# Identity products in the opening of a two-block transformer kernel, a first weight part made by GpSimd, and weight parts moved at two hand-overs

## The chip, the cores and the metric

One NeuronCore of a Trainium2 chip runs the whole program. Its engines are TensorE (PE, matmul), VectorE (DVE), ScalarE (ACT), GpSimd (POOL) and SyncE (SP, which here only issues DMAs). The metric is the device time of one execution in microseconds. The kernel before takes 1233.42 us, the median of three runs (1233.16, 1233.42 and 1234.23).

## The reference

Two transformer blocks in float32 over 256 tokens of 1024 features, cut here to what sets the order of the work. The first block has two layers, the second has one.

```python
def first_block(...):
    for i in range(2):
        h = rms_norm(x, g[0])
        m = neighborhood_attention(h, ...) if i == 0 else diff_attention(h, ...)
        x = x + rms_norm(m, g[1])
        f = conv_glu_ffn(rms_norm(x, g[2]), ...)       # D_FF = 2816
        x = x + rms_norm(f, g[3])
        gate = sigmoid(rms_norm(x, g[4]) @ ple_w_gate[i])
        x = x + gate * (p[i] @ ple_w_proj[i])

def second_block(...):                                  # one layer
    h = h + 0.5 * swiglu(rms_norm(h), w1_gate, w1_up, w1_down)
    u = rms_norm(h) @ w_in                              # HGRN2 mixer and latent attention
    h = h + concat([o_hg, o_mla]) @ w_out
    h = h + 0.5 * swiglu(rms_norm(h), w2_gate, w2_up, w2_down)
    h = h + sigmoid(rms_norm(h) @ w_ple_gate) * (p @ w_ple_proj)
    return rms_norm(h, ln_final)
```

## The kernel before

The 256 tokens are two tiles of 128 (t = 0 and 1), and the 1024 features are 8 blocks of 128. The layers run as ten phases, numbered 0 to 9: `na, ffn, ple, da, ffn, ple, glu, mix, glu, ple`. Phase 0 is the neighborhood attention, phase 2 the gate of layer 0, phase 3 the differential attention, phase 4 the FFN after it. The order of every engine's work is written out by hand; counting semaphores tie the engines together.

**Weights.** They are cut into slabs of 1 MB (128 partitions by 2048 elements), numbered through the program. A slab passes four steps. SP issues its DMA into one of 3 `raw` buffers (L524); a buffer is free once the low part of the slab three before it is made (`lo_done`). ACT rounds it to fp32r, the high part `w_hi` (`feed`, L691). DVE subtracts that from the raw values, the low part `w_lo` (`feed`, L1249, or in two halves, `feed_half`, L1257). PE multiplies: each product of float32 accuracy is three fp32r products, high by high, high by low and low by high (L1939 to L1941). `w_hi` and `w_lo` are rings of 5 slabs. An engine's `feed(n)` makes every slab below number n that it has not made yet. `hi_done` counts high parts, `lo_done` low parts.

**Activations.** A tile is normalized in this way: ACT squares and sums it (`pre` before a stage, `post` after one, L695), GpSimd turns the sums into 1/rms (`powers`, L562 to L571), DVE multiplies by it (`normed`, L1288, two instructions of 512 columns), PE transposes the 8 blocks against the identity (`turn_x`, L1996), and then ACT and DVE make the high and the low part of each block (`tile_parts`, L698 and L1271). In `tile_parts` ACT's step i waits for DVE's step i - 2, and step i of DVE waits for that of ACT, so the two alternate. In phases whose rms factor is applied later (4 among them) `turn_x` transposes x itself.

**The opening.** PE runs 16 identity products into a bank that nobody reads (L2601), turns the first gain row (L1961, copied out by DVE at L1860), then both tiles (`turn_x(0, 0)` and `(0, 1)`), and enters `first_columns` (L2108: high part of slab 0 by both parts of the tokens, 2 columns groups of 16 matmuls; L2113: its low part, 16 matmuls), then `half_columns(0, 2)`, `(0, 3)`, scores, taps and `value_rows`. DVE runs: gain copy, `normed(0, 0)`, steps 0 to 3 of tile 0, `normed(0, 1)`, steps 4 to 7, tile 1, `feed(2)` (slabs 0 and 1), `lambdas` and `rotary` (some 4.4 us of small instructions), slab 2, then in `attention0` `expand(0)` (waits for the DMA of the relative-position table), `scores(0, 0)`, `expand(1)`, `taps_out` and slab 3. ACT runs the four squares, steps 0 to 3 of tile 0, slab 0, steps 4 to 7, tile 1, slabs 1 and 2. GpSimd issues late gain rows, makes both 1/rms, sets 32 columns of `invf` (L588, which `rotary` waits for) and, once `hi_done` is 2, issues the DMAs of the table (L579).

**Hand-over from phase 2 to phase 3.** PE makes the last gate quarter in two pieces with `turn_x(3, 0)` between them, and then runs `value_rows(3, 0, 0, 0)` and `(3, 0, 1, 0)` (12 products each on tile 0, four blocks each, waiting for each block's low part), `turn_x(3, 1)` and `value_rows` on tile 1. With b the first gate slab, slabs b+4 and b+5 are those of these value rows, and slab b+6 that of the first columns. `add_gated(2, n)` (DVE, L1324 and L1325) adds gate piece n to x; `gates(2, n)` (ACT, L742) makes its sigmoid. Pieces 2 to 4 belong to tile 1 and end in `pre(3, 1)`.

**End of phase 3.** With b the first slab of phase 3, b+12 to b+15 are those of the output projection, b+16 to b+18 the first three of the FFN. After the last two units of attention (6 and 7) DVE scales the outputs (`scaled_outputs(3, 1)`, L1489 and L1493, which waits for GpSimd's 1/rms of these units, L570 and L571), PE turns them (`output_turn(3, 1)`, L1961), ACT and DVE split them (`output_parts(3, 1)`), and PE runs the second half of the projection, `output_piece(3, 1, t, half)`. ACT's `post(3, 0)` follows its slabs up to b+18; then come the rms factor, `post_added` (DVE, L1314) and `turn_x(4, 0)`, which PE runs before the last 6 products of the projection.

## Time and profile before

| | |
|---|---|
| median of three runs | 1233.42 us (1233.16 to 1234.23) |
| the profiled execution | 1234.14 us, of which the span in the trace is 1232.4 us |
| PE busy | 1210.2 us, 98% of the span |
| DVE busy | 943.8 us, 77% |
| ACT busy | 674.5 us, 55% |
| POOL busy | 135.1 us, 11% |
| DMA | 214.52 MB, mean 174 GB/s |
| chain that ended last | PE 91%, DVE 4%, ACT 3%, DMA 1% |

Times inside the trace are microseconds from the start of the span. A group's idle time before it is named with what ended it. PEclk is the granted TensorE clock: 1.00 is 2.4 GHz, 0.50 is 1.2 GHz. A matmul's record is longer than its distance to the next, since matmuls are pipelined.

### The profile page before, as it was taken

Reading aid. Unit: us, or ns where it says so; the run is one execution under the profiler, and the core shown is the slowest. Engines: PE = TensorE matmul, PEld = TensorE weight load, DVE = VectorE, ACT = ScalarE, POOL = GpSimd, SP = SyncE. Lnnn points to the kernel's source line nnn. Section 1 sums busy time; section 2 is a strip of 40 time slices with the busy share of each in tenths; the row PEclk is TensorE's granted clock in tenths of the full one; section 3 lists DMA queues with packets and bytes.
Section 4 is the critical chain, followed back from the end, with each engine's and each line's share of the span. In section 5 each row is a group of like instructions: output and inputs, shape, how many; then the busy total and the mean of one; then the engine's idle time right before and its main releaser. Section 6 shows DMA issues by size and latency. Waiting matters only on the chain.

```text
span 1232.4 us, 17869 instructions
## 1 busy us (share of the span) xinstructions
PE 1210.2 (98%) x6977; PEld 1054.8 (86%) x6977; DVE 943.8 (77%) x1272; ACT 674.5 (55%) x1064; POOL 135.1 (11%) x256
## 2 busy tenths in 40 slices
PE   7999999999989998999999999999999999999997
PEld 7889888888879887888888988888897888888886
DVE  6757699888866577998888898766776778677665
ACT  6656654444576776444445855444586555344435
POOL 4000330000120001000001200000207410000002
PEclk8999999999999999999999999999999999999999
DMA  8834376565444434666654575566455136655540
GB/s 254 243 135 140 117 250 202 189 205 191 151 154 169 140 133 133 207 206 202 205 178 165 164 245 177 192 205 197 138 178 171 35 105 228 205 188 188 193 149 35
DMA packets 149015, 214.52 MB, mean 174 GB/s; under 512 B 4410, under 2 KB 114428, under 8 KB 148932
## 3 DMA queue, kind: packets, MB, share of 16 engines
q1 hardware_dynamic: 145596, 205.39, 50.7%
q0 software_dynamic: 1632, 4.71, 1.5%
q10 hardware_dynamic: 1704, 3.28, 0.8%
q8 instruction: 56, 0.92, 0.3%
q14 instruction: 27, 0.22, 0.1%
HBM read 212.30 MB, written 1.06 MB: 173 GB/s over the span
## 4 chain that ended last, share of the span: by engine, by line
PE 91%; DVE 4%; ACT 3%; DMA 1%; issue 1%; POOL 0%; POOLq 0%; ACTq 0%; DVEq 0%
PE work L2340 24%; PE work L2343 12%; PE acc L1939 9%; PE acc L1940 9%; PE acc L1941 9%; PE work L1939 5%; PE work L1940 5%; PE work L1941 5%; PE work L2149 2%; PE work L1961 2%; PE acc L2125 1%; PE work L2329 1%; PE work L2317 1%; PE work L2331 1%; ACT w_hi L691 1%; DVE w_lo L1249 1%
## 5 line engine op out<-in xcount | busy, mean ns | idle before, releaser
L1249 DVE TENSOR_TENSOR w_lo<-raw,w_hi 128x2048 fp32r<-128x2048 f32 (+1 forms) x192 | 435.7, 2276 | 45.7 <-ACT w_hi L691 45.7
L691 ACT ACTIVATE w_hi<-raw 128x2048 fp32r<-128x2048 f32 x195 | 369.0, 1899 | 71.2 <-PE work L2343 60.0
L2340 PE MATMUL work<-hT_both,w_hi 128*128 128x512 f32 x1280 | 318.8, 391 | 0.0
L2340 PEld LDWEIGHTS work<-hT_both,w_hi 128*128 128x128 f32 x1280 | 234.8, 188 | 45.1
L2343 PEld LDWEIGHTS work<-hT_both,w_lo 128*128 128x128 f32 x1280 | 174.6, 190 | 12.5
L2343 PE MATMUL work<-hT_both,w_lo 128*128 128x256 f32 x1280 | 178.5, 282 | 0.0
L1939 PE MATMUL acc<-w_hi,aux_hi 128*128 128x512 f32 x400 | 157.9, 395 | 0.0
L1940 PE MATMUL acc<-w_lo,aux_hi 128*128 128x512 f32 x400 | 156.7, 392 | 0.0
L1941 PE MATMUL acc<-w_hi,aux_lo 128*128 128x512 f32 x400 | 155.8, 390 | 0.0
L1036 ACT ACTIVATE aux_hi<-Z 128x256 fp32r<-128x256 f32 x88 | 37.0, 420 | 195.2 <-DVE Z L1664 107.3
L1635 DVE TENSOR_REDUCE Z<-work 128x256 f32<-128x512 f32 x88 | 60.6, 689 | 90.4 <-PE work L2343 88.6
L1941 PEld LDWEIGHTS acc<-w_hi,aux_lo 128*128 128x128 f32 x400 | 75.1, 188 | 16.5
L1939 PEld LDWEIGHTS acc<-w_hi,aux_hi 128*128 128x128 f32 x400 | 75.4, 189 | 13.8 <-issue 0.3
L1940 PEld LDWEIGHTS acc<-w_lo,aux_hi 128*128 128x128 f32 x400 | 75.5, 189 | 12.1
L562 POOL TENSOR_SCALAR ms<-ssq 128x1 f32<-128x1 f32 x26 | 18.4, 709 | 555.2 <-ACT xn L695 442.3
L1939 PE MATMUL work<-hT_both,w_hi 128*128 128x256 f32 x272 | 78.5, 289 | 0.0
L1940 PE MATMUL work<-hT_both,w_hi 128*128 128x256 f32 x272 | 76.9, 283 | 0.0
L1941 PE MATMUL work<-hT_both,w_lo 128*128 128x256 f32 x272 | 76.9, 283 | 0.0
L828 ACT ACTIVATE Z<-work 128x512 f32<-128x512 f32 (+1 forms) x92 | 45.6, 516 | 51.8 <-PE work L1941 37.0
L1939 PE MATMUL acc<-w_hi,hT_both 128*128 128x512 f32 (+1 forms) x184 | 68.3, 371 | 0.8 <-DVE hT_both L1271 0.8
L1941 PE MATMUL acc<-w_hi,hT_both 128*128 128x512 f32 (+1 forms) x184 | 66.9, 363 | 0.0
L1940 PE MATMUL acc<-w_lo,hT_both 128*128 128x512 f32 (+1 forms) x184 | 66.8, 363 | 0.0
(260 smaller groups left out, 1814.4 us busy)
## 6 DMA issues: line engine op xcount, KB each, us to landing
raw<-in_ffn_w_in SPq DMA_DIRECT2D x44, 1024.0 KB, 5.1
raw<-in_ffn_w_out SPq DMA_DIRECT2D x22, 1024.0 KB, 5.0
raw<-in_w_gate SPq DMA_DIRECT2D x22, 1024.0 KB, 5.3
raw<-in_w_up SPq DMA_DIRECT2D x22, 1024.0 KB, 5.3
raw<-in_w_down SPq DMA_DIRECT2D x22, 1024.0 KB, 5.0
raw<-in_na_w_qkv SPq DMA_DIRECT2D x12, 1024.0 KB, 7.3
raw<-in_da_w_qkv SPq DMA_DIRECT2D x12, 1024.0 KB, 5.2
raw<-in_ple_w_gate SPq DMA_DIRECT2D x8, 1024.0 KB, 5.2
```

The costliest lines, as they stand in the source:

```text
L691: act.activation(w_hi[:, n % RING, 0:size], raw[:, n % RAW, 0:size], ACT.Copy).then_inc(hi_done, 1)
L828: act.activation(dst, src, func).then_inc(bank_free[g % WORK], 1)
L1036: act.activation(aux_hi[:, c % 2, :], hid32[:, c % 2, :], ACT.Copy).then_inc(hid_hi_done, 1)
L1249: dve.tensor_tensor(w_lo[:, n % RING, 0:size], raw[:, n % RAW, 0:size], w_hi[:, n % RING, 0:size].bitcast(F32), ALU.subtract).then_inc(lo_ ...
L1635: dve.tensor_reduce(src, bank(g).rearrange("p (e s) -> p s e", e=2), AX.X, ALU.add)\
L1939: pe.matmul(dst, stationary[0], moving[0], start=first, stop=False)
L1940: pe.matmul(dst, stationary[0], moving[1], start=False, stop=False)
L1941: return pe.matmul(dst, stationary[1], moving[0], start=False, stop=last)
L1961: ins = pe.transpose(b[0:width, i * P:i * P + rows], v, ident[0:rows, 0:rows])
L2149: ins = pe.matmul(b[:, (2 * j + a) * n:(2 * j + a + 1) * n], wt[:, cols(2 * k + a)], vtok[:, k, c0:c0 + n], start=k == 0, stop=k == 1)
L2340: pe.matmul(b.rearrange("p (e s) -> p e s", e=2), v[0][:, k, cols(c % 2)], hT_both[:, k, :, :], start=k == 0, stop=False)
L2343: ins = pe.matmul(b[:, 0:S], v[1][:, k, cols(c % 2)], hT_hi[:, k, :], start=False, stop=k == KT - 1)
```

## The change

GpSimd makes the high part of slab 0 once it has landed, between its second 1/rms and the `invf` columns; ACT leaves it out, runs the 16 steps of both tiles in one piece, and goes on with slabs 1 and 2. PE's 16 identity products become 10 ahead of the gain row, 5 behind it, 8 behind `turn_x(0, 0)` and 2 behind `turn_x(0, 1)`, now written to a work bank. At the hand-over from phase 2 to 3 DVE makes the low part of slab b+4 ahead of the two `add_gated`, that of slab b+5 whole ahead of the steps of tile 0 instead of in two halves among them, runs these 8 steps in one piece, and adds gate pieces 2 to 4 behind them; ACT runs the 8 steps in one piece and then `gates(2, 4)` and `pre(3, 1)`. At the end of phase 3 ACT makes the high part of slab b+15 in two halves, before each of the last two `weights_turned`, and DVE makes its low part whole ahead of `scaled_outputs(3, 1)` instead of in halves behind it.

```diff
@@ gpsimd, opening @@
             powers("pre0.1")
+            pool.wait_ge(landed[0], 16)
+            pool.tensor_copy(w_hi[:, 0, :], raw[:, 0, :]).then_inc(hi_done, 1)
             for i in range(32):
@@ scalar @@
+            def feed_half(i):
+                n = fed[0]
+                size = slabs[n][1] * slabs[n][2] // 2
+                half = slice(i * size, (i + 1) * size)
+                act.wait_ge(landed[n % RAW], 16 * (n // RAW + 1))
+                if n >= RING:
+                    released(act, n - RING)
+                ins = act.activation(w_hi[:, n % RING, half], raw[:, n % RAW, half], ACT.Copy)
+                if i == 1:
+                    ins.then_inc(hi_done, 1)
+                    fed[0] += 1
@@ scalar, gated_end(2) @@
-                    tile_parts(3, 0, range(4))
+                    tile_parts(3, 0)
                     gates(2, 4)
-                    pre(3, 1, (0,))
-                    tile_parts(3, 0, range(4, 6))
-                    pre(3, 1, (1,))
-                    tile_parts(3, 0, range(6, 8))
-                    pre(3, 1, (2,))
+                    pre(3, 1)
                     feed(b + 7)
                     tile_parts(3, 1)
@@ scalar, attention3 @@
                 unit_exps(3, 7)
+                feed_half(0)
                 weights_turned(3, 6)
+                feed_half(1)
                 weights_turned(3, 7)
@@ scalar, opening @@
-            tile_parts(0, 0, range(4))
-            feed(1)
-            tile_parts(0, 0, range(4, 8))
+            tile_parts(0, 0)
             tile_parts(0, 1)
+            act.wait_ge(hi_done, 1)
+            fed[0] = 1
             feed(3)
@@ vector, gated_end(2) @@
+                    feed(b + 5)
                     add_gated(2, 0)
                     add_gated(2, 1)
-                    feed(b + 5)
                     normed(3, 0)
-                    feed_half(0)
-                    tile_parts(3, 0, range(4))
+                    feed(b + 6)
+                    tile_parts(3, 0)
                     add_gated(2, 2)
                     add_gated(2, 3)
-                    tile_parts(3, 0, range(4, 6))
                     add_gated(2, 4)
-                    feed_half(1)
-                    tile_parts(3, 0, range(6, 8))
                     normed(3, 1)
                     tile_parts(3, 1)
@@ vector, attention3 @@
-                feed(b + 15)
+                feed(b + 16)
                 scaled_outputs(3, 1)
-                feed_half(0)
                 output_parts(3, 1)
-                feed_half(1)
                 feed(b + 18)
@@ tensor @@
-            def keep_busy(n, dst):
+            def keep_busy(n):
                 for _ in range(n):
-                    pe.matmul(dst[:, 0:384], ident[:, :], causal[:, :], start=True, stop=True)
+                    pe.matmul(work[:, WORK - 1, 0:P], ident[:, :], ident[:, :], start=True, stop=True)
...
-            for _ in range(16):
-                pe.matmul(acc[:, 2, 0:P], ident[:, :], ident[:, :], start=True, stop=True)
+            keep_busy(10)
             pe.wait_ge(first_row, 16)
             turn(G["vec"], [vrow[0:KT, :]])
+            keep_busy(5)
             turn_x(0, 0)
+            keep_busy(8)
...
                         turn_x(0, 1)
+                        keep_busy(2)
                         attention0()
```

## Rows read from the trace of the kernel before

**Rows 1.** The page's busy times; one of PE's waits: total, times, longest.
```profile
PE 1210.2 (98%) x6977; PEld 1054.8 (86%) x6977; DVE 943.8 (77%) x1272; ACT 674.5 (55%) x1064; POOL 135.1 (11%) x256
...
PE work L1939 <- DVE hT_both L1271: 2.9, 4, 1.5
```
**Rows 2.** Windows of the opening: length, busy by engine, PEclk, DMA share, GB/s.
```profile
9.80:11.70 1.90, 0.00 (x0) 0.00 (x0) 1.69 (x6) 1.77 (x4) 0.00 (x0) 1.00 1.01 272
14.80:20.00 5.20, 5.20 (x24) 5.20 (x25) 4.67 (x9) 4.88 (x8) 1.02 (x2) 0.50 0.42 136
```
**Rows 3.** Timeline of the opening: start, duration, engine, line, tiles, idle before.
```profile
6.43 0.57 POOL L567 TENSOR_TENSOR rstd<-ms,mhalf 128x1 f32<-128x1 f32 x1
...
8.08 0.88 DVE L1288 TENSOR_SCALAR xn<-x,rstd 128x512 f32<-128x512 f32 x2
...
10.80 1.90 ACT L691 ACTIVATE w_hi<-raw 128x2048 fp32r<-128x2048 f32 x1
11.20 0.88 DVE L1288 TENSOR_SCALAR xn<-x,rstd 128x512 f32<-128x512 f32 x2
...
12.99 0.61 DVE L1271 SCALAR_TENSOR_TENSOR hT_both<-acc,vecT,hT_both 128x128 fp32r<-128x128 f32 x2 [0.91 <-ACT hT_both L698]
...
17.19 4.48 DVE L1249 TENSOR_TENSOR w_lo<-raw,w_hi 128x2048 fp32r<-128x2048 f32 x2
...
21.11 2.08 PE L2113 MATMUL work<-hT_both,w_lo 128*128 128x256 f32 x16
...
34.42 2.28 DVE L1249 TENSOR_TENSOR w_lo<-raw,w_hi 128x2048 fp32r<-128x2048 f32 x1
...
37.47 0.39 PE L1939 MATMUL work<-w_hi,hT_both 128*128 128x512 f32 x1
```
**Rows 4.** GpSimd's largest copy and a tiny one; slab 0's landing after its issue.
```profile
L673 POOL COPY Z<-Z 128x256 f32<-128x256 f32 x1 | 0.4, 393 | 0.0
...
L616 POOL COPY Z<-tT 8x9 f32<-8x9 f32 x1 | 0.2, 183 | 0.0
...
DMA to landing us min/median/max: 7.3/7.3/7.3
```
**Rows 5.** Timeline of phase 7: GpSimd and DVE side by side.
```profile
962.50 2.02 POOL L642 TENSOR_TENSOR Z<-Z 128x1024 f32<-128x1024 f32 x1 [1.23 <-DVE Z L1754]
963.60 1.47 DVE L1753 TENSOR_TENSOR Z<-Z 128x512 f32<-128x512 f32 x1
```
**Rows 6.** Timeline of the hand-over from phase 2 to phase 3.
```profile
347.99 0.69 DVE L1324 TENSOR_TENSOR xn<-xn,Z 128x512 f32<-128x512 f32 x1 [3.45 <-ACT xn L742]
...
351.66 1.43 POOL L562 TENSOR_SCALAR ms<-ssq,ms 128x1 f32<-128x1 f32 x1 [0.84 <-ACT xn L695]
...
354.32 1.09 PE L1996 MATMUL acc<-ident,xn 128*128 128x128 f32 x8 [0.80 <-DVE xn L1288]
...
362.61 0.50 PE L1939 MATMUL work<-w_hi,hT_both 128*128 128x512 f32 x1 [1.49 <-DVE hT_both L1271]
...
363.13 0.88 DVE L1288 TENSOR_SCALAR xn<-x,rstd 128x512 f32<-128x512 f32 x2 [0.32 <-POOL rstd L567]
...
367.69 0.47 PE L1939 MATMUL work<-w_hi,hT_both 128*128 128x512 f32 x1 [0.50 <-DVE hT_both L1271]
```
**Rows 7.** Timeline of the end of phase 3.
```profile
459.00 0.19 POOL L570 TENSOR_SCALAR ms<-ssq 128x2 f32<-128x2 f32 x1 [7.33 <-ACT work L858]
...
461.08 0.17 DVE L1489 TENSOR_TENSOR grow<-rstd,rinv 128x8 f32<-128x8 f32 x1 [3.00 <-POOL rstd L571]
...
466.09 1.22 DVE L1257 TENSOR_TENSOR w_lo<-raw,w_hi 128x1024 fp32r<-128x1024 f32 x1
...
472.53 1.92 ACT L691 ACTIVATE w_hi<-raw 128x2048 fp32r<-128x2048 f32 x1 [5.06 <-DMA raw<-in_ffn_w_in]
...
477.62 1.96 PE L1996 MATMUL acc<-ident,x 128*128 128x128 f32 x8 [2.92 <-DVE x L1314]
```
**Rows 8.** A window behind that wait (columns as in rows 2).
```profile
477.60:481.00 3.40, 3.38 (x12) 3.09 (x13) 2.99 (x6) 2.90 (x10) 2.12 (x4) 0.51 0.04 17
```

## The prediction

> **What bounds the kernel now.** I read the page first: PE is busy for 98% of the span [rows 1], so time can only be won where PE idles, where its clock is low, or where it runs work that is not needed. PE's waits come next. The list is short, and two entries lie where this change works: 2.9 us for low parts [rows 1], most of it at the start of phase 3 [rows 6], and a single wait of 2.92 us in front of phase 4 [rows 7]. The third place is the opening, where the windows show something that the waits don't: PE idled 1.9 us from 9.80 at full clock, and all of the 5.2 us from 14.80 to 20.00 ran at the lower level, 1.2 GHz [rows 2]. The reader should then take the timeline of each of these three places and ask which engine is late, and behind what it stands in its own queue. Everything between the three places is work that PE starts and the others follow, so a gain made at one should be carried to the end; I found no transfer there that is tied to the clock on the wall rather than to PE.
>
> **The opening, old chain.** DVE holds it: it ran `normed(0, 1)` at 11.20, then waited 0.91 us for ACT, which was busy with slab 0's high part from 10.80 for 1.90 us; steps 4 to 15 ran from 12.99, and the low part of slab 0 from 17.19 [rows 3]. Everything that DVE does up to the low part of slab 3 (ended 34.42 + 2.28 = 36.70) follows in a row. PE first needs that slab at 37.47, so this chain has 0.77 us to spare there, 0.7 after a semaphore's delay [rows 3].
>
> **GpSimd's copy.** Slab 0 lands 7.3 us after its issue at 1.71, at 9.0 [rows 4], when GpSimd has just finished its second 1/rms. The trace has no copy of 128x2048 on GpSimd. The nearest is 128x256 in 393 ns [rows 4]. Scaled by elements that is 3.1 us; a copy of 9 elements takes 0.183 us, so that is the fixed part, and 0.18 + 2048 x (0.393 - 0.183)/247 is 1.92 us. Ends: 1.92 and 3.1 us, and twice 1.92 if writing fp32r costs GpSimd more than float32. I take 1.92, because the two rows differ as a fixed part and a rate would have it: the copy runs from 9.0 to 11.0. PE needs it only at about 13.5, so by itself it costs nothing; if that cover went it would cost its overrun.
>
> **What it collides with.** While GpSimd ran a `tensor_tensor` from 962.50 to 964.52, a DVE `tensor_tensor` with both operands in SBUF took 1.47 us from 963.60, where its like take 0.69: it stood until GpSimd was through [rows 5]. The other way round, GpSimd's tiny `ms` took 1.43 us from 351.66 while DVE made a low part until 352.94 [rows 6]. So DVE's `normed(0, 1)` may be held until 11.0. Without the collision it would start at 10.2: the gain row was turned behind 16 products, before 8.08 [rows 3], and behind 10 it is turned some 2 us earlier (unless its own DMA is later, which no row shows), before the 1/rms is there at 6.43 + 0.57 = 7.00, so that `normed(0, 0)` goes at 7.05 instead of 8.08, and all behind it 1.0 us earlier [rows 3].
> The rows show the collision for DVE instructions with two SBUF operands, and `normed` has one. The Trainium skill (SBUF — State Buffer, "SBUF: two separate sides") says that the pair of ports which GpSimd and VectorE share is an exclusive lock, held for a whole instruction, and counts a VectorE instruction in a 2-port mode to those that need it. By that rule `normed`, at 0.88 us for two where `tensor_tensor` takes 0.69 each, is held; it speaks against the change, since what GpSimd takes off ACT it takes partly from DVE. No row here shows it for a single operand.
>
> **The opening, sum.** Held, `normed(0, 1)` starts at 11.0, 0.2 earlier; and behind it the 0.91 us wait for ACT is gone, so step 4 runs at 11.85 instead of 12.99: 1.15 us earlier for all that DVE does, the low part of slab 0 at about 16.05 instead of 17.19. ACT, its last step 1.15 earlier, makes slabs 1 and 2 earlier by as much, GpSimd then issues the table's DMAs (it waits for `hi_done` 2) and SP slab 3 (it waits for `lo_done` 1) 1.15 earlier too, so the wait of `expand(0)` shrinks alike. PE: the last 16 products of L2108 and the 16 of L2113 at 0.13 us each [rows 3] put it through first_columns at 16.05 + 0.25 + 2.0 + 2.0 = 20.3 instead of 23.1, 2.8 us earlier, and it would then stand in front of slab 3: the gain of the place is 1.15 + 0.7 = 1.8 us. Not held, it is 0.8 more, 2.6. If the clock is low all the same, PE takes 32 x 0.24 from 13.6 instead of from 14.8 and gains 0.5 to 2.0, by when the clock returns (in the trace it returned 5.4 us after matmuls began at 14.8). The identity products themselves lie in PE's idle time: 8 of them at 0.22 us fill 1.8 of the 1.9 us that PE idled at 9.80 [rows 2], and at the low clock 3.1 us, which would push `turn_x(0, 1)` to 11.6, where `normed` has it anyway. GpSimd's `invf` columns move behind the copy, to 12.3; `rotary` wants them after 20. Nobody waits.
>
> **Hand-over from phase 2 to 3.** DVE sat idle 3.45 us before 347.99 [rows 6]; slab b+4's low part (2.28 us, high part ready at 345.95) now fills it, and ends 0.3 us after the gate piece is ready, so the adds come 0.3 later. But behind them DVE is free, and GpSimd's 1/rms is not held: 351.05 (x ready) + 0.8 (square) + 0.1 + 0.28 + 0.08 + 0.57 gives 352.9, against 353.74. PE's idle 0.80 us in front of `turn_x(3, 0)` [rows 6] is gone. Slab b+5's low part then runs whole from 353.85 to 356.1, the 8 steps of tile 0 (0.79 us a pair, as in the opening) to 359.1. PE comes at 357.3 and takes 0.69 us a block, in time with them, so the two `value_rows` run through to 362.85; the waits of 0.5 and 1.49 us at 359.7 and 361.1 [rows 6] go. What is late next: the three gate adds, moved behind the steps, end at 362.2, `pre(3, 1)` at 362.85, the 1/rms at 363.9. `normed(3, 1)`, at 363.13 before [rows 6], runs at 364.0; PE waits from 362.85 to 364.5, turns, and starts tile 1 at 364.5 + 1.54 = 366.05 instead of 367.69 [rows 6]: 1.6 us. SP's next slabs are issued 4.7 and 6 us earlier, which nothing here needs. ACT's slab b+6 ends at 364.8, just before the turned block, so it costs nothing.
>
> **End of phase 3.** The wait of 2.92 us in front of `turn_x(4, 0)` has a long root. ACT stood 5.06 us for a DMA until 472.53, and `post(3, 0)` stood behind it in ACT's queue [rows 7]. That slab, b+18, is issued when the low part of b+15 is done, which came in a half at 466.09 + 1.22 = 467.3 [rows 7]; 467.3 + 5.2 is the landing. Now DVE makes it in the 3.00 us that it sat idle before 461.08 [rows 7], from 458.05 to 460.35, if the high part is there: ACT's two halves (half of 1.90 each, 1.05) fit its idle times around the two `weights_turned`, which move by 0.1. So the slab is issued 6.9 us earlier and lands by 466, and ACT has it rounded at 469.5. `post(3, 0)` then waits for PE alone (its second half of tile 0 at 470.8), and with the old distances (square, 1/rms, add, 3.6 us from square to turn) the turn could start at 473.7, while PE gets to it at 474.7. The wait goes: 477.62 - 474.54 = 3.1 us. Behind it PE ran from 477.6 to 481.0 at half clock [rows 8]: 1.7 us more, which go with it.
> The price: the low part holds GpSimd's `ms` of units 6 and 7 (459.00 [rows 7]) to 460.45, the 1/rms comes 1.25 us later, `scaled_outputs` runs at 462.3 instead of 461.08. PE reached its turn at 463.08 anyway and now stands 0.2; ends 0 and 0.6 us. Place: 3.1 + 1.7 - 0.2 = 4.6 us.
>
> **Sum.** 1.8 + 1.6 + 4.6 = 8.0 us against the profiled execution's 1234.14, so 1226.1; the median before is 0.7 lower than that execution, which gives 1225.4. I write 1225.5.
>
> **Rivals.**
> - *The clock falls elsewhere.* PE now idles 1.65 us and then 0.65 us around the turn of tile 1 in phase 3. It kept its clock over an idle of 1.49 [rows 6], and lost it over 3.08 [rows 7, 8] and in the opening, where an idle stretch of 1.9 us [rows 2] was followed by another behind one transpose. The new gap lies between. Price: as at 477.6, 1.7 us. If the opening doesn't keep its clock either, 1.3 more. 1227.1 to 1228.5.
> - *GpSimd's copy is long, or holds DVE's steps too.* At 3.1 to 3.9 us it ends at 12.1 to 12.9, `normed(0, 1)` with it, and the opening's gain is (3.7 - copy) us: 0.6 to -0.2, so 1226.7 to 1227.5. If it holds DVE's steps 0 to 3 as well, another 1.3 us: up to 1228.8.
> - *`normed` is not held.* The opening gives 2.6: 1224.7.
> - *Slab b+18 stays late* (ACT's halves don't fit, so that the low part falls behind `scaled_outputs`): 3.4 us in all, 1230.
> - *Slower.* One mechanism: the same copy, very slow. From 3.7 us on each us of it is a us lost, since DVE's whole chain stands behind `normed(0, 1)`. To eat the other 6.2 us it has to last 9.9 us, and 12.4 to be seen, 6 ns an element, where the row has 1.5 with its fixed part [rows 4]. At 15 us: 1225.5 + 1.8 + 11.3 = 1238.6.
>
> **How the numbers follow.** The forecast with its small terms (1224.9 to 1226.4): 0.5. `normed` not held: 0.12. The clock: 0.18. The copy: 0.12. Slab b+18 late: 0.05. Slower: 0.02. The remaining 0.01 is between. The range takes in the forecast, the unheld case, the clock and most of the copy: 1223.0 to 1229.3. About 0.2% (2.5 us) is what a measurement of this kernel can tell from no change; the first four cases are further below (0.92), and of the late slab, which gives just over it, I count 0.02 as faster and 0.03 as same: faster 0.94, same 0.04 with the 0.01 between, slower 0.02.
>
> **What would show it.** GpSimd's copy at 9.0 for 2 us, and `normed(0, 1)` starting where it ends; PEclk at 1.00 through `first_columns`, and then a wait of PE for slab 3's low part near 34.5. In phase 3 no wait inside the first value rows, a new one of 1.6 us at the turn of tile 1. At the end of phase 3 no wait of ACT for a DMA, a short wait of PE in front of the output turn, none before `turn_x(4, 0)`, PEclk 1.00 behind it. Wrong would be: a copy of over 3.5 us, PEclk of 0.50 in either place, or a gain that PE hands back as a new wait in phase 0 or 4.

## The result and the profile after

The changed kernel takes 1225.2 us (median of 4 executions, 1225.2 to 1227.99) beside 1233.29 us of the kernel before on the same chip (1232.58 to 1234.23): a ratio of 0.994, 95% interval 0.9922 to 0.9957. Forecast were 1225.5 us. The profiled execution took 1227.99 us, with a span of 1226.3; what its 2.8 us over the other three are is the first question below.

The waits of PE answer to [rows 1]. Columns: engine, tile and line that waited, whom for; us in total, times, longest.

```profile
PE acc L2003 <- DVE xn L1300: 2.6, 2, 1.5
...
PE work L2448 <- ACT pts L838: 1.2, 1, 1.2
PE work L1946 <- DVE hT_both L1283: 1.0, 2, 0.5
...
PE acc L2132 <- ACT Z L838: 0.5, 1, 0.5
```

Gone are the 2.9 us in front of phase 4 and two of the four waits of the value rows (the four were 2.9 us, the two left are 1.0). New are 1.2 us for `pts` (0.7 before) and 0.5 us of L2132, the first scores.

Windows of the changed kernel, which answer to [rows 2] and [rows 8]: length, busy by engine (PE, PEld, DVE, ACT, POOL), PEclk, DMA share, GB/s.

```profile
9.80:11.70 1.90, 0.55 (x5) 0.36 (x4) 1.90 (x3) 0.65 (x2) 1.90 (x9) 1.00 0.98 268
13.90:18.80 4.90, 4.84 (x33) 4.25 (x34) 4.37 (x9) 4.58 (x8) 0.72 (x1) 1.00 0.62 215
...
470.90:474.30 3.40, 3.40 (x25) 3.11 (x24) 2.61 (x7) 2.96 (x12) 1.82 (x5) 1.00 0.31 123
...
940.00:942.00 2.00, 1.65 (x9) 1.65 (x10) 1.97 (x3) 0.30 (x1) 2.00 (x1) 0.70 0.00 0
942.00:944.00 2.00, 2.00 (x8) 1.35 (x7) 1.00 (x4) 1.08 (x4) 1.93 (x2) 0.50 0.92 224
```

`first_columns` (13.90 to 18.80) and the start of phase 4 (470.90) run at full clock, 2.4 GHz, where both ran at 1.2 before. The last two rows are new: at 940 the clock falls, in the middle of phase 7, which the change doesn't touch.

Timeline of the opening, answering to [rows 3]: start, duration, engine, line, tiles, idle before and its releaser.

```profile
9.61 1.89 POOL L588 CAST w_hi<-raw 128x2048 fp32r<-128x2048 f32 x1 [0.99 <-DMA raw<-in_na_w_qkv]
...
10.05 2.12 DVE L1300 TENSOR_SCALAR xn<-x,rstd 128x512 f32<-128x512 f32 x2
12.10 0.60 DVE L1283 SCALAR_TENSOR_TENSOR hT_both<-acc,vecT,hT_both 128x128 fp32r<-128x128 f32 x2
...
13.88 4.94 PE L2115 MATMUL work<-hT_both,w_hi 128*128 128x256 f32 x32 [0.51 <-DVE hT_both L1283]
...
27.32 1.13 PE L2132 MATMUL acc<-Z 64*128 64x256 f32 x8 [0.50 <-ACT Z L838]
33.26 2.28 DVE L1261 TENSOR_TENSOR w_lo<-raw,w_hi 128x2048 fp32r<-128x2048 f32 x1
```

GpSimd's copy took 1.89 us (forecast 1.92). The slab landed at 9.6 instead of 9.0. `normed(0, 1)`, 0.88 us before, took 2.12 and ended 0.67 after the copy: held. The low part of slab 3 is 1.16 earlier than at 34.42.

The two places of phase 3, answering to [rows 6] and [rows 7].

```profile
351.82 1.08 PE L2003 MATMUL acc<-ident,xn 128*128 128x128 f32 x8
352.06 2.29 DVE L1261 TENSOR_TENSOR w_lo<-raw,w_hi 128x2048 fp32r<-128x2048 f32 x1
...
361.82 0.88 DVE L1300 TENSOR_SCALAR xn<-x,rstd 128x512 f32<-128x512 f32 x2 [1.68 <-POOL rstd L567]
362.37 1.09 PE L2003 MATMUL acc<-ident,xn 128*128 128x128 f32 x8 [1.13 <-DVE xn L1300]
363.96 0.47 PE L1946 MATMUL work<-w_hi,hT_both 128*128 128x512 f32 x1 [0.50 <-DVE hT_both L1283]
...
454.31 2.29 DVE L1261 TENSOR_TENSOR w_lo<-raw,w_hi 128x2048 fp32r<-128x2048 f32 x1
455.31 1.33 POOL L570 TENSOR_SCALAR ms<-ssq 128x2 f32<-128x2 f32 x1 [7.33 <-ACT work L868]
458.51 0.17 DVE L1498 TENSOR_TENSOR grow<-rstd,rinv 128x8 f32<-128x8 f32 x1 [1.92 <-POOL rstd L571]
462.16 3.71 ACT L693 ACTIVATE w_hi<-raw 128x2048 fp32r<-128x2048 f32 x2
465.77 0.58 ACT L709 ACTIVATE Z<-acc 128x512 f32<-128x512 f32 x1
470.94 1.03 PE L2003 MATMUL acc<-ident,x 128*128 128x128 f32 x8
```

No wait inside the first value rows, one of 1.13 at the turn of tile 1 (362.37). At the end ACT rounds two slabs in a row at 462.16 without waiting for a DMA (5.06 us before), and PE turns phase 4's block at 470.94 with no wait.

**Where the time went, by segments.** One table carries the rest of this document. Each row is the profiled execution of one kernel; each column but the last is the distance between two rows of its timeline. The opening goes from ACT's first square of x (at 4.41 to 4.78, by when x landed) to `turn_x(1, 0)`; the hand-over from there to the turn of tile 1 in phase 3; the end of 3 to `turn_x(4, 1)`; the next to the first product of `pts` in phase 7 (L2441 before, at 948.12, L2448 in the changed kernel); the fifth to the end of the span. The last column is the time of that profiled execution.

| kernel | opening | hand-over | end of 3 | to phase 7 | to the end | us |
|---|---|---|---|---|---|---|
| before | 134.80 | 226.79 | 118.50 | 463.47 | 284.28 | 1234.14 |
| changed | 133.35 | 224.56 | 113.93 | 464.05 | 285.95 | 1227.99 |
| changed, again | 132.64 | 224.50 | 113.88 | 463.46 | 284.27 | 1224.94 |
| opening alone | 132.94 | 226.71 | 118.55 | 463.48 | 284.21 | 1232.17 |
| hand-over alone | 133.81 | 224.51 | 117.90 | 463.47 | 284.30 | 1230.13 |
| end of phase 3 alone | 135.69 | 226.75 | 113.85 | 463.64 | 284.34 | 1230.61 |
| identity products alone | 133.64 | 226.78 | 118.45 | 463.47 | 284.18 | 1232.78 |
| copy alone | 134.64 | 226.76 | 118.28 | 463.43 | 284.17 | 1233.57 |
| changed, old identities | 134.28 | 224.56 | 113.92 | 463.44 | 284.22 | 1226.85 |
| changed, no copy | 133.20 | 224.56 | 115.24 | 463.37 | 284.25 | 1227.14 |
| changed, old opening | 133.76 | 224.49 | 113.87 | 463.38 | 284.24 | 1225.90 |
| changed, long copy | 134.39 | 224.51 | 113.87 | 463.40 | 284.23 | 1226.88 |
| changed, pieces | 132.93 | 224.48 | 113.87 | 463.36 | 284.24 | 1225.34 |
| changed, head only | 134.16 | 224.51 | 113.93 | 463.42 | 284.30 | 1226.61 |

The hand-over takes one of two values to within 0.1, whatever the company. So does the end of phase 3 to within 0.3, but for two rows where the clock went another way (117.90, 115.24), and the columns of phase 7 and the end stand still to within 0.3 but for the first profile of the changed kernel. Only the opening moves freely: the four profiles of the old opening lie at 133.76 to 135.69, the three of the new one at 132.64 to 133.35. The ranges don't overlap, and their means are 1.5 apart.

The runs below were made in four rounds, each beside the kernel before (medians 1233.69, 1233.86, 1234.71 and 1234.34 us). Across rounds the ratios are the measure; a difference of two medians from different rounds carries the 1.0 us by which these four differ.

### The profile page after: what moved, and what is told of

Same layout as the page of the kernel before. It is cut to its first block, busy times and chain, and to the rows that moved or that the text cites. A ratio compares the mean times of both kernels' runs of the same rounds, so it can differ in the third digit from the quotient of the medians.

```text
span 1226.3 us, 17906 instructions
## 1 busy us (share of the span) xinstructions
PE 1210.3 (99%) x6995; PEld 1054.3 (86%) x6995; DVE 945.3 (77%) x1270; ACT 672.6 (55%) x1064; POOL 138.0 (11%) x257
## 4 chain that ended last, share of the span: by engine, by line
PE 90%; DVE 5%; ACT 2%; DMA 1%; issue 1%; POOL 0%; POOLq 0%; ACTq 0%; DVEq 0%
PE work L2347 24%; PE work L2350 12%; PE acc L1946 10%; PE acc L1947 10%; PE acc L1948 10%; PE work L1946 5%; PE work L1947 5%; PE work L1948 5%; DVE w_lo L1261 2%; PE work L2156 2%; PE work L1968 2%; PE acc L2132 1%; PE work L2336 1%; PE work L2324 1%; PE work L2338 1%; PE work L2461 1%
## 5 line engine op out<-in xcount | busy, mean ns | idle before, releaser
L1261 DVE TENSOR_TENSOR w_lo<-raw,w_hi 128x2048 fp32r<-128x2048 f32 (+1 forms) x194 | 440.4, 2277 | 47.9 <-ACT w_hi L693 47.9
L693 ACT ACTIVATE w_hi<-raw 128x2048 fp32r<-128x2048 f32 (+2 forms) x193 | 365.2, 1899 | 69.3 <-PE work L2350 59.2
```

The lines of the kernel that those rows point to most:

```text
L693: act.activation(w_hi[:, n % RING, 0:size], raw[:, n % RAW, 0:size], ACT.Copy).then_inc(hi_done, 1)
L1261: dve.tensor_tensor(w_lo[:, n % RING, 0:size], raw[:, n % RAW, 0:size], w_hi[:, n % RING, 0:size].bitcast(F32), ALU.subtract).then_inc(lo_ ...
```

## The experiments

**The changed kernel again, and its three places one by one.** The first run repeats the kernel; the others undo two of three places each, so one diff stands for each.

> The changed kernel once more, unaltered, for a second profile and for how its time spreads. The first profile of it shows a granted clock of 0.50 for some 3.4 us in phase 7 (from about 940), and 1227.99 us, where three unprofiled runs show 1225.2. Theory: the clock's fall in phase 7 is what the profiled execution had and the others had not, so that an execution without it has a span near 1223.5 and a time of 1225.2, with the opening, the hand-over and the end of phase 3 as in the first profile. Rival: the profile itself costs the 2.8 us, and each profiled execution shows 1228 whatever the clock does.

Measured: 1225.22 us (1224.94, 1227.09, 1225.07, 1225.36). The profiled execution is the one of 1224.94 us, and phase 7 shows what the first profile lost (windows of the repeated run):

```profile
940.00:942.00 2.00, 2.00 (x11) 1.15 (x9) 1.54 (x5) 1.44 (x5) 1.93 (x2) 1.00 0.58 133
942.00:944.00 2.00, 2.00 (x15) 1.52 (x14) 1.08 (x2) 0.14 (x2) 1.93 (x3) 1.00 1.06 377
```

Full clock there, 463.46 and 284.27 in the table as before the change. Of the 3.05 us between the two profiled executions 0.71 lie in the opening and 0.59 + 1.68 in phase 7, where `pts` came late and the clock fell. The theory holds. Why `pts` came late can be followed back in the two traces, first profile, then repeat, which stands 0.83 earlier from phase 4 on:

```profile
924.58 1.92 ACT L693 ACTIVATE w_hi<-raw 128x2048 fp32r<-128x2048 f32 x1 [1.64 <-DMA raw<-in_w_out]
...
929.09 0.86 DVE L1760 TENSOR_TENSOR Z<-Z 128x512 f32<-128x512 f32 x1 [3.83 <-ACT Z L1113]
```

```profile
923.39 1.92 ACT L693 ACTIVATE w_hi<-raw 128x2048 fp32r<-128x2048 f32 x1 [1.31 <-DMA raw<-in_w_out]
...
927.90 0.71 DVE L1760 TENSOR_TENSOR Z<-Z 128x512 f32<-128x512 f32 x1 [3.50 <-ACT Z L1113]
```

A slab of `w_out` landed 0.33 later, and two DVE instructions beside a long row of GpSimd instructions took 0.15 and 0.09 longer; `pts` is 0.6 later, and PE waits 1.24 us for it instead of 0.67. That the clock fell 0.5 us behind the end of this wait is seen once. Two of the eight executions lie at 1227 or above; the others at 1224.9 to 1225.4. The second of the two (1227.09, mean clock 0.997) has no profile.

The edit of the first is the part of the change in the opening, of the second that in `ph == 2`, each as in the diff above; the third is, on DVE and on ACT:

```
-                feed(b + 15)
+                feed(b + 16)
                 scaled_outputs(3, 1)
-                feed_half(0)
                 output_parts(3, 1)
-                feed_half(1)
...
+                feed_half(0)
                 weights_turned(3, 6)
+                feed_half(1)
                 weights_turned(3, 7)
```

> The kernel before with the edits of the opening alone. Theory (the opening's gain, worked out beforehand as 1.8 us and read in the changed kernel's trace at the turn of phase 1 as 1.55 us, is carried to the end): 1231.6 us. Rival (the gain is handed back by a later wait of PE, in phase 2 to 3 or in phase 7): 1232.8 to 1233.3 us.

> The kernel before with the hand-over from phase 2 to 3 alone. Forecast: 1.6 us faster, 1231.7. From the changed kernel's trace (where the place gains 2.18 us): 1231.1. A rival has part of the 2.18 come from the opening's edits, through earlier slabs: then 1231.7 here too. PE's wait at the turn of tile 1 should be 1.1 to 1.7 us, and none inside the first value rows.

> The kernel before with the edits at the end of phase 3 alone. Theory (the slab b+18 lands earlier, the wait of 3.1 us in front of the turn goes and with it 3.4 us at half clock, 1.7 us): 4.6 us faster, 1228.7. Rival (the wait goes, but the clock falls somewhere behind it all the same): 1230.3. In the trace ACT has no wait for a DMA near 467, and the granted clock is 1.00 from 470 to 485.

Measured, medians of 10 executions each: opening 1233.21 us, ratio 0.9996 (0.9986 to 1.0005); hand-over 1231.0, 0.9979 (0.997 to 0.9988); end 1230.21, 0.9972 (0.9962 to 0.9981). Together 0.5 + 2.7 + 3.5 = 6.7 us, where the whole change gives 8.5 in this comparison (the kernel before: 1233.69).

The hand-over hit its 1231.1. The other two missed their theories (1231.6 and 1228.7) and came out at the numbers of their rivals (1232.8 to 1233.3, and 1230.3), but not by the rivals' mechanisms, as the table shows. The hand-over segment shrinks by 2.28 alone and by 2.2 to 2.3 in company, the end by 4.65 alone and by 4.6 in company: both add up, and PEclk is 1.00 from 470 to 485 in the run with the end alone. With the opening alone no later column hands its gain back. Its executions fall in two groups by their mean granted clock: the four at 0.997 or 0.998 took 1231.5 to 1232.2, as the theory had it (the profiled one is among them), the six at 0.995 or 0.996 took 1232.8 to 1235.7. Where the clock fell in these six no profile shows.

The 0.6 us that the hand-over alone gains in the next column is clock, as these rows show, the first two of the hand-over alone, the last of the kernel before:

```profile
474.25 1.32 PE L2001 MATMUL acc<-ident,x 128*128 128x128 f32 x8 [2.96 <-DVE x L1322]
480.63 1.18 PE L2001 MATMUL acc<-ident,x 128*128 128x128 f32 x8
```

```profile
484.65 1.18 PE L1996 MATMUL acc<-ident,x 128*128 128x128 f32 x8
```

The hand-over alone waits 2.96 us in front of phase 4, as the kernel before did, but keeps its clock, and from `turn_x(4, 0)` to `turn_x(4, 1)` it takes 6.38 us, where the kernel before took 7.03 (477.62 to 484.65) and the changed kernel 5.36. So the half clock costs 0.65 there; the other 1.0 goes with the late DVE, which PE follows: its turn takes 1.32 us instead of 1.03, and it waits 0.48 for a step of DVE behind it.

The opening of the run with the end alone took 135.69, 0.89 more than that of the kernel before, with the same instructions. In its profile that is the loss, and it isn't the end's.

**What sets the old opening.** PE's timeline from the head to the gain row's turn, first of the end alone, then of the changed kernel with the old opening (its diff below); both issue the same 16 products, which are 32 rows.

```profile
1.58 6.61 PE L2613 MATMUL acc<-ident 128*128 128x128 f32 x32 [1.58 <-POOL ident L544]
8.13 0.22 PE L1973 MATMUL work<-ident,Z 8*128 8x8 f32 x1
```

```profile
1.58 5.32 PE L2606 MATMUL acc<-ident 128*128 128x128 f32 x32 [1.58 <-POOL ident L544]
6.83 0.22 PE L1966 MATMUL work<-ident,Z 8*128 8x8 f32 x1
```

The same 32 rows take 6.61 or 5.32 us, by when in the execution they become faster. Two windows of the end alone, whose PEclk doesn't tell them apart:

```profile
0.00:7.30 7.30, 5.72 (x27) 5.72 (x28) 0.00 (x0) 3.94 (x9) 5.29 (x17) 1.00 0.76 250
7.30:8.20 0.90, 0.90 (x8) 0.78 (x7) 0.00 (x0) 0.00 (x0) 0.72 (x3) 1.00 1.11 351
```

A row takes 0.21 us up to 7.30 and 0.11 behind it; with the old opening in the changed kernel 17 rows take 3.42 us up to 5.00, and 19 take 2.00 behind it. I read this as the first rise of the clock. The gain row's turn stands behind these rows, `normed(0, 0)` behind that, and the whole chain of DVE. In the six profiles with the old head the turn came at 6.83 to 8.13. But the later gain row is the smaller part of the 0.89 us. In the end alone it puts `normed(0, 0)` 0.3 later behind ACT's first square than in the kernel before, and there GpSimd's fills had just begun (GpSimd, then DVE):

```profile
8.37 0.98 POOL L588 MEMSET Z<- 128x1 f32 x32
```

```profile
8.47 1.54 DVE L1302 TENSOR_SCALAR xn<-x,rstd 128x512 f32<-128x512 f32 x2
```

It takes 1.54 us instead of 0.88, its first instruction 1.15 instead of 0.48, and ends that one 0.27 behind the last fill. In the kernel before it came at 8.08, ahead of them.

```
-            # the four keep_busy lines (10, 5, 8 and 2 products)
+            for _ in range(16): pe.matmul(acc[:, 2, 0:P], ident, ident)
-            pool.tensor_copy(w_hi[:, 0, :], raw[:, 0, :]).then_inc(hi_done, 1)
```

This diff is shortened; ACT's part of the opening is undone too.

> The changed kernel without its opening: 16 identity products at the head, slab 0's high part on ACT, both places of phase 3 as changed. It says what the whole opening is worth in the company of the other two, where the opening alone had shown 0.5 us of the median. Theory A (the opening's 1.6 to 2.3 us of turn_x(1, 0) are kept to the end when the later falls of the clock don't come): 1225.2 + 2.0 = 1227.2 us, within 0.4. Theory B (the parts add up as they do alone, 0.5 + 2.7 + 3.5 us, and the rest of the changed kernel's 8.5 us is something that only all three bring): about 1227.5 to 1228 here and an opening worth more than its trace shows. The clock should fall in the opening for 6.8 us as in the kernel before, and turn_x(1, 0) stand where it stood there.

Measured: 1226.43 us (1225.61 to 1226.99), ratio 0.9938 (0.9923 to 0.9953). Both theories had it slower (1226.8 to 1228). Between medians of two rounds the opening is worth 1.2 us in the company of the others, by the ratios nothing. The profiled execution is one with an early rise, and turns its gain row at 6.83. The interval is that of the changed kernel in its own repeat (0.9938, 0.9923 to 0.9953): differences of about a us between kernels of this study are not resolved by the ratios. What is said of them below rests on the segments of single profiles, and on the executions, which hardly overlap (1225.6 to 1227.0 here, 1224.4 to 1225.7 in the run with the pieces, which shared the chip).

**Identity products or copy.** The identity products are PE's part of the opening's edits, the copy is GpSimd's and ACT's. Two runs add one of them to the kernel before, two take one of them out of the changed kernel.

> The kernel before with the identity products of the opening alone (10, 5, 8 and 2 of them in place of 16); ACT makes slab 0's high part as before, and both places of phase 3 stay old. Theory A (the earlier gain row moves the chain, GpSimd's copy adds little): normed(0, 0) goes at 6.93 as in the changed kernel, ACT ends its first steps near 9.8 and makes slab 0 from 9.8 to 11.7, DVE's step 4 runs at 12.05, 0.95 us before the 12.99 of the kernel before; with the clock kept turn_x(1, 0) comes 1.6 us earlier. Theory B (it is the copy that lets step 4 go, as the prediction had it): step 4 stays near 12.9, and the place gives only what the clock gives, 0.7 us. Of the end: 1232.1 us by A and 1233.0 by B where the clock keeps its other levels, and up to 1.7 more in executions in which a further stretch of 3.4 us falls to half clock, as the opening alone showed (1231.5 to 1235.7).

> The kernel before with GpSimd's copy of slab 0 alone, behind the old 16 identity products; both places of phase 3 stay old. normed(0, 0) stays at 8.08, the copy runs from 8.9 to 10.8 and is over before normed(0, 1) at 11.2, so DVE isn't held: normed(0, 1) takes 0.88 for two. Theory (the copy's whole worth is the wait of 0.91 us for ACT): step 4 at 12.1 instead of 12.99, the clock falls in the opening as before, turn_x(1, 0) 0.9 us earlier, 1232.8 us. Rival (PE at half clock sets the place, so the earlier steps bring nothing): the same 1233.7 as before.

> The changed kernel with the old 16 identity products and none in the gaps; GpSimd's copy and both hand-overs stay. Theory (the identity products are worth 0.8 us at DVE by the earlier gain row, and the clock of the opening): normed(0, 0) back at 8.08, the opening at half clock from about 13 for some us, PE no longer early at slab 3; turn_x(1, 0) 1 to 1.4 us later than in the changed kernel, 1226.3 to 1226.6 us. Rival (slab 3's low part sets the place whatever the clock): only DVE's delay of 0.7, 1225.9.

> The changed kernel with slab 0's high part on ACT again; identity products and both hand-overs stay. By the trace of the changed kernel (ACT ends its first steps at 9.8 to 10.5, step 4 of DVE at 11.4 to 12.1): ACT makes the slab from 9.8 to 11.7, step 4 runs at 12.05, DVE's normed(0, 1) takes 0.88 unheld. Theory A (the copy is worth what ACT's queue adds beyond the held normed): 0.0 to 0.7 us later than the changed kernel, 1225.2 to 1225.9. Theory B (the prediction: the copy takes away a wait of 0.91 us): 0.9 later, 1226.1 or more.

Measured: identity products alone 1232.76 us, 0.9992 (0.9983 to 1.0001); copy alone 1233.72, 0.9999 (0.9989 to 1.0008), beside 1233.86 of the kernel before; the changed kernel with the old identities 1226.47, 0.994 (0.9925 to 0.9955), without the copy 1226.73, 0.9941 (0.9924 to 0.9957). By the ratios the changed kernel misses neither by more than 0.4 us (0.9938 in its repeat, with its interval around all three), by medians of different rounds by 1.2 and 1.5; alone the identities give 1.1 and the copy 0.1. With the identities alone, step 4 runs at 11.87 although ACT makes the slab, 1.12 earlier than in [rows 3]; theory A of that run holds for DVE's chain, but not for the clock: PE idled 1.52 us in front of `first_columns`, and PEclk is 0.53 from 15.90 to 19.40, identity products or not. Behind the same 1.52 us the run without the copy kept its clock. The copy alone came out at its rival's number (1233.7) and has its surprise in three rows (DVE, then GpSimd):

```profile
10.81 1.72 DVE L1302 TENSOR_SCALAR xn<-x,rstd 128x512 f32<-128x512 f32 x2
...
9.05 1.89 POOL L588 CAST w_hi<-raw 128x2048 fp32r<-128x2048 f32 x1 [0.45 <-DMA raw<-in_na_w_qkv]
10.89 0.97 POOL L590 MEMSET Z<- 128x1 f32 x32
```

`normed(0, 1)` came 0.13 before the copy's end and was expected to go unheld. Its first instruction took 1.33 us, past the copy and past all of the 32 `invf` fills behind it, which the change had moved there: it ended 0.28 behind the last. So the copy alone gave step 4 only 0.5 us, and slab 3 landed late on top (ACT waited 2.28 us for it, and PE 0.48 for its low part).

Without the copy the time is that of theory B (1226.1 or more), but the chain shows theory A and loses little: step 4 stands 7.39 behind ACT's first instruction, with it 6.93 (again) and 7.64 (the first profile, slab landed late). In the profile 1.3 us more are a fall of the clock at 364.6 for 3.4 us, right behind the turn of tile 1: 115.24 in the table instead of 113.9. The window of it:

```profile
364.60:368.00 3.40, 3.40 (x10) 2.60 (x9) 3.14 (x7) 3.26 (x7) 0.00 (x0) 0.50 0.01 2
```

This is the place that the prediction's rival named. Whether leaving out the copy brings that fall or it fell by chance is open; the executions' mean clocks (0.997, 0.999, 0.997, 0.996) say that it isn't there in all. The one at 0.999 took 1226.32 us all the same, 1.1 over the repeat's median in the round before, which this fall doesn't explain.

**The head or the gaps.**

```
             keep_busy(10)
             turn(G["vec"], [vrow[0:KT, :]])
-            keep_busy(5)
             turn_x(0, 0)
-            keep_busy(8)
-                        keep_busy(2)
```

> The changed kernel with 10 identity products at the head and none in the gaps (5 behind the gain row's turn, 8 and 2 behind the first two turns left out). Against the changed kernel it gives the worth of the gap products alone, against the run without identity products (1226.5, 16 at the head) the worth of the shorter head. Theory A (the shorter head is what counts: in the runs so far the head's products ended between 6.9 and 8.2 us, by when the clock rose, and the gain row waited for them; with 10 it is turned before its 1/rms is there in any case): normed(0, 0) near 2.5 us behind ACT's first instruction as in the changed kernel, step 4 at 6.9 to 7.6 behind it, turn_x(1, 0) at 132.7 to 133.5, 1225.2 to 1225.7 us even where first_columns runs partly at half clock, since slab 3's low part is DVE's. Theory B (the gap products' clock counts as well): a stretch of 3.4 or 6.8 us of half clock from about 12, PE past slab 3's landing place by 0.3 to 1.2 us, 1225.9 to 1226.5 us.

Measured: 1227.79 us (1225.87 to 1229.62), ratio 0.9951 (0.9937 to 0.9965). The median is above what both theories said: by medians of different rounds 2.6 us over the changed kernel, by the ratios 1.6, with intervals that overlap (0.9937 to 0.9965 and 0.9923 to 0.9953). In the profile the opening is 0.8 to 1.5 longer (134.16 against 133.35 and 132.64). The windows:

```profile
9.00:13.00 4.00, 1.73 (x8) 1.57 (x8) 3.69 (x11) 2.31 (x8) 3.16 (x33) 0.54 0.94 288
13.00:16.00 3.00, 2.92 (x13) 2.42 (x12) 2.01 (x7) 2.24 (x8) 0.00 (x0) 0.50 1.06 386
```

PE had idled 1.33 and 2.58 us around `turn_x(0, 0)`; the clock fell at 9.3 and stayed at 1.2 GHz for 6.8 us. With the gap products the same windows show 1.00. The profiled execution has its gain row early all the same, so the low clock shows in the turn of the second block (1.97 us instead of 1.09), for which a step of DVE then waits 0.50, and in `first_columns`, 5.54 us instead of 4.93. That is 0.6 of the 1.5 us: PE is at its first scores 22.77 behind ACT's first square, 22.15 in the repeat. The other 0.9 comes behind them, and isn't the clock. Slab 3 landed late (ACT, then PE):

```profile
29.44 1.92 ACT L693 ACTIVATE w_hi<-raw 128x2048 fp32r<-128x2048 f32 x1 [1.96 <-DMA raw<-in_na_w_qkv]
```

```profile
36.68 0.51 PE L1946 MATMUL work<-w_hi,hT_both 128*128 128x512 f32 x1 [0.55 <-DVE w_lo L1261]
```

ACT waited 0.88 us for this slab in the repeat, and PE none for its low part. So theory B's mechanism is there, at 0.6 us in one profile; the rest of the median's loss is not shown to come from the gap products.

**The lock.** The copy twice as long in one instruction, and cut into four:

```
-            pool.tensor_copy(w_hi[:, 0, :], raw[:, 0, :]).then_inc(hi_done, 1)
+            pool.tensor_copy(w_hi[:, 0:2, :], raw[:, 0:1, :].broadcast_to([P, 2, 2048])).then_inc(hi_done, 1)
```

> The changed kernel with GpSimd's copy made twice as long in one instruction: it writes slab 0's high part and, from the same source, as much again into the place of slab 1's, which ACT overwrites later. Theory (the copy holds DVE's normed(0, 1) to its end): by 1.89 us for 2048 elements it takes 3.6, ends near 12.6 instead of 10.8, normed(0, 1) ends near 13.2 instead of 11.45, and everything of DVE to slab 3's low part is 1.75 later; of that PE gets 1.3 to 1.75, so 1226.5 to 1227.0 us; the prediction's (3.7 - copy) gives 1.7. Rival (a one-operand normed runs beside the copy and was late for another reason): normed ends by 11.5, the high part is late for first_columns alone, under 0.5 us, 1225.2 to 1225.7.

Measured: 1227.38 us (1226.88 to 1227.93), ratio 0.9945 (0.9931 to 0.9958), 2.2 over the changed kernel. GpSimd, then DVE:

```profile
9.12 3.60 POOL L588 CAST w_hi<-raw 128x4096 fp32r<-128x4096 f32 x1 [0.26 <-DMA raw<-in_na_w_qkv]
...
10.30 3.09 DVE L1300 TENSOR_SCALAR xn<-x,rstd 128x512 f32<-128x512 f32 x2
13.31 0.60 DVE L1283 SCALAR_TENSOR_TENSOR hT_both<-acc,vecT,hT_both 128x128 fp32r<-128x128 f32 x2
```

`normed` ends 0.67 behind the copy, as at 1.89 us of copy, and step 4 follows: the theory's mechanism holds (the median is 0.4 above its range), and an instruction with one SBUF operand is held. Steps 0 to 3, which read PSUM, ran beside the copy from 8.95 in 1.44 us, as without it. The Trainium skill (SBUF — State Buffer, "SBUF: two separate sides") says so of the 2-port modes, and the trace agrees, with 2.12 and 3.09 us for 0.88; the mode itself is in no trace. The (3.7 - copy) of the prediction is right in slope: 1.71 us more of copy cost 1.75 in the opening segment (134.39 against 132.64).

```
-            pool.tensor_copy(w_hi[:, 0, :], raw[:, 0, :]).then_inc(hi_done, 1)
+            for q in range(4): ins = pool.tensor_copy(w_hi[:, 0, q*512:(q+1)*512], raw[...])
+            ins.then_inc(hi_done, 1)
...
             act.activation(trig, rot, ACT.Sin).then_inc(trig_ready, 1)
+            columns_out(0, 2)
             act.wait_ge(lam_sum, 1)
```

> The changed kernel with two edits. GpSimd's copy is made in four instructions of 512 columns, so that DVE's normed(0, 1) can get in between; and ACT copies the bank c0.2 out between its Sin and its Exp, where it now does so behind the Exp's table, for which PE stood 0.5 us in front of the first scores. If a lock is held for one instruction: normed(0, 1) is held 0.6 us at most (a quarter is some 0.55 to 0.6) and ends near 11.1 instead of 11.45 to 12.2, step 4 as much earlier. The wait of 0.5 us in front of the scores goes. PE had 0.5 us of slack at slab 3's low part, so both together give 0.5 (the column) plus what the pieces give DVE, 0.2 to 0.5: 1224.3 to 1224.7 us. Rival 1: GpSimd keeps the port for its whole row of pieces (as its copy and the 32 memsets behind it did to normed in the run with the copy alone), and only the column counts: 1224.8. Rival 2: the exps and slab 3's low part, which hang on the table of biases (its DMA is issued when slab 1 is rounded), set the place, and the freed 0.5 us comes back as a wait of PE for slab 3: 1225.2.

Measured: 1225.23 us (1224.44 to 1225.71), ratio 0.9926 (0.9914 to 0.9939), rival 2's number: by its time no better than the changed kernel, 0.5 to 0.9 short of what was expected:

```profile
9.23 2.48 POOL L590 CAST w_hi<-raw 128x512 fp32r<-128x512 f32 x4 [0.35 <-DMA raw<-in_na_w_qkv]
...
10.32 1.66 DVE L1303 TENSOR_SCALAR xn<-x,rstd 128x512 f32<-128x512 f32 x2
...
26.55 1.13 PE L2135 MATMUL acc<-Z 64*128 64x256 f32 x8
...
35.62 0.50 PE L1949 MATMUL work<-w_hi,hT_both 128*128 128x512 f32 x1 [0.31 <-DVE w_lo L1264]
```

Four pieces take 2.48 us instead of 1.89 (605 to 803 ns each), and `normed` got in late: 829 and 912 ns for its two instructions, ended at 11.98, 0.27 behind the last piece (one copy from 9.23 would have let it end at 11.8). The wait of the scores is gone (no bracket at 26.55), and 0.31 of it is back as a wait for slab 3's low part at 35.62: mostly rival 1, then rival 2.

## Why the prediction was right

The time was (1225.5 forecast, 1225.2 measured), and so was the mechanism of all three places. Its terms had these sizes:

- **End of phase 3, 4.6 us forecast: 4.6 measured** (118.50 to 113.9, and 4.65 alone). The root was the late slab: with its low part in DVE's idle stretch, ACT's 5.06 us for a DMA, PE's 2.92 and the half clock behind it went together. The split of the sum is less good than the sum: 2.9 came up to `turn_x(4, 0)` as forecast and 1.67 behind it, but of these the clock is 0.65 by the run with the hand-over alone, where the forecast gave it all 1.7; the rest is the wait on DVE's late pieces, which the sum didn't name. GpSimd's `ms` was held as forecast (455.31, 1.33 us instead of 0.19). The hand-over alone shows the coupling from the other side: it still has a wait of 2.96 us there.
- **Hand-over, 1.6 forecast: 2.3 measured.** Mis-sized was the end of DVE's chain. Shifted by the opening's 1.55, the slab's low part starts at 353.61 (forecast 353.85), the adds end at 361.69 (362.2), `normed(3, 1)` goes at 363.37 (364.0), and PE's new wait is 1.13, not 1.65. The 0.6 is a row of roundings up, each 0.1 to 0.3.
- **Opening, 1.8 forecast: 1.45 and 2.16 in two profiles, 1.5 between the means of all profiles with and without it.** Neither medians nor ratios resolve it. The copy, the held `normed`, step 4 (11.85 forecast; 12.10 and 11.38) and the kept clock stood as written. Two steps failed. The gain of 1.15 was put down to the wait of 0.91 for ACT that the copy takes away; by the run without it, step 4 loses 0.46 at most, and it is the earlier gain row that moves the chain. And the old opening was read from one execution: its gain row came at 7.74, where the runs with the same head had 6.83 to 8.13, and the `invf` fills, for which nobody was said to wait, can hold `normed(0, 0)` there for 0.7 us. Also, PE was said to stand next for slab 3's low part; it stood 0.5 us for ACT's evacuation in front of the first scores, which took up that slack (slab 3 came 1.16 earlier, PE 1.56).
- **The rival of the clock came in at least one of eight executions**, with its price (1227.1 to 1228.5 forecast, 1227.99 measured); a second lay at 1227.09, unprofiled. In the changed kernel's profile it came in another place than the turn of tile 1 (where the run without the copy had it): in phase 7, behind a wait for `pts` of 1.24 us instead of 0.7. The prediction had looked for new gaps only where the change makes them. The prediction ordered the cases by the length of PE's idle stretch, and that alone doesn't tell: the hand-over alone kept its clock behind 2.96 us, the first profile of the changed kernel lost it behind 1.24.
- **The other rivals.** The unheld `normed` is refuted, the late slab too (no wait of ACT for a DMA). The long copy wasn't there, and the run with 3.60 us shows that its price was right and that it doesn't hold DVE's steps.

The measured terms of the repeated run, 2.16 + 2.29 + 4.62 = 9.07 us, are nearly all that separates it from the profiled execution before (the sums of their rows in the table are 9.09 apart). Between medians it is 8.5, since the profiled execution before lies 0.5 above the median of its kernel and that of the repeat 0.3 below its own.

## What to carry to other kernels

Cut the timeline into segments at the same instruction in every variant before comparing totals: two of the three places here added up to 0.1 us, and the medians alone would have said that they don't. Products meant to keep TensorE's clock up have to stand in the gaps: without them the opening lost its clock for 6.8 us, which cost 0.6 us in the one profile. They are no guarantee: with them in place one of seven profiles lost it for 3.4 us. When a variant comes out slower than its mechanism allows, look for a late DMA before blaming the edit. Before a step is moved from one engine to GpSimd, look at what VectorE runs beside it, and at what else GpSimd issues right behind.

## What was not expected of the hardware

- Products at the head become faster at different times in executions with the same head, read here as the first rise of TensorE's clock, and work queued behind them inherits it: 32 rows took 5.32 to 6.61 us.
- A run of 32 tiny GpSimd fills (0.97 us in all) kept a waiting VectorE instruction out like one long instruction: 1.33 us for a first instruction of `normed` of 0.48 in the run with the copy alone, 1.15 in that with the end alone.
- A longer GpSimd instruction is cheaper than pieces: 0.88 ns an element at 4096 (3.60 us), 0.92 at 2048 (1.89), 1.19 at 512 (0.61, the median of four).
- Slab 3's landing varies: from SP's issue to ACT's start on it 9.7 us in the repeated run and 10.3 before, but 11.1 with the old opening and 10.8 with the head only, where ACT waited 1.69 and 1.96 us for it. What delays it is open; it is one part of the opening's spread, beside the gain row and the fills.
